# Gated DeltaNet heads: three GpSimd products taken out of the scan, and other places for weight splits and block copies

## The chip, the cores and the metric

One core of a Trainium2 chip. The metric is the device time of one execution in microseconds, the median over several. Five engines run their own instruction streams side by side and wait for each other through semaphores: TensorE (PE, matrix products), VectorE (DVE), ScalarE (ACT), GpSimd (POOL) and SyncE (SP), which here only issues transfers.

## The reference

One inference step of a hybrid network with two layers that share their shapes, over 512 latent and 128 context tokens of width 1024. A layer normalises its input, scales and shifts it, projects it, and hands the projection to four branches of four heads each: A (gated DeltaNet), B (Hyena convolution), C (neighbourhood attention), D (differential attention). Their outputs are gated, projected, merged and projected again. The change is in branch A alone:

```python
def gdn_chunked(q, k, v, g, beta, s0):
    gc = jnp.cumsum(g..., axis=-1)
    decay = jnp.where(incl, jnp.exp(gc_i - gc_j), 0.0)
    kb = k * beta
    lower = jnp.where(strict, einsum('id,jd->ij', kb, k) * decay, 0.0)
    sol = triangular_solve(lower + eye, concatenate([v * beta, kb * exp(gc)]))
    u, w = sol[..., :dv], sol[..., dv:]
    a_intra = jnp.where(incl, einsum('id,jd->ij', q, k) * decay, 0.0)
    q_dec, k_dec, g_last = q * exp(gc), k * exp(gc_last - gc), exp(gc_last)
    def step(s, xs):
        v_new = u_i - w_i @ s
        o_i = q_i @ s + a_i @ v_new
        s = s * gl_i + k_i.T @ v_new
        return s, o_i
```

q and k pass a width-3 convolution, SiLU and an L2 norm; v a convolution and SiLU. Each head runs it in both directions of the sequence (d = 0, 1), with initial states per head, and the final context states are an output.

## The kernel before, in words

Everything is written out by hand, engine by engine; no planner reorders it. Tokens are five tiles of 128 (four latent, one context); a chunk in the kernel is a tile. All large projections go through blocks of 128 output channels (8 x 128 x 128 weights, 512 KB). SP loads a block into one of two raw buffers (`stream`), ScalarE makes its rounded upper part (`split_hi`, called `A_hi` in branch A), VectorE the rest (`split_lo`, `A_lo`), and TensorE makes three products per piece (upper times upper, upper times rest, rest times upper) into one of two PSUM buffers `proj` (L794). A block of branch A is cut into eighths, which `eighths`, `fill` and `part` put as filling between the small steps of the Delta heads. A load waits until both splits of the block two before are done, a split until TensorE is through with the block two before it.

**A head** has four blocks (q, k, v, gate) and these stages. *Front* (units u = 0 to 9, TensorE into `mix`, ScalarE out of it, `A_front` on both): u 0 to 2 turn the log-decays and ScalarE makes `decT` = exp(-|gc_i - gc_j|) for both directions, 128 x 1280; u 3 to 5 turn k and q into token order and sum their squares; u 5 to 7 make the Gram products k k^T and k q^T (`gram`); u 8, 9 turn v. *Masks and blocks*: GpSimd's `A_front` takes the inverse roots of the sums of squares (`stat`, L600) and scales beta by them; then it makes three products of 128 x 1280: `dec` = decT * beta * rn^2, decT * triangle (L617), and that times the Gram matrix of q (L623). VectorE's `A_decays` and `A_blocks` cut the 16 x 16 diagonal blocks out (four 32 x 320 products each, into D32, then `C16`), and `A_lower` multiplies `dec` by the Gram matrix of k. *Block inverses*: the blocks travel by small transfers (`blocks_in`; tiles 0 to 2 through SP's queue in `relay`, tiles 3 and 4 through GpSimd's) to 40 partitions, where VectorE inverts all 16 x 16 blocks (`A_scaled`, `A_pivots` 1 to 14, `A_inverse`), and back (`inverses_back`). VectorE spreads direction 0 and ScalarE direction 1 into X and Y (`A_spread`). *Levels*: the inverse grows from 16 to 32 to 64 to 128 in steps on TensorE (`A_level_q`, `A_level_d`, `A_mid_q`, ...), each answered by ScalarE (`A_level`, `A_mid`, `A_last`) and VectorE (`update`, `update_mid`, `update_last`). *Scan*: five steps, `A_scan` on TensorE, ScalarE's copy of v (`vn`), VectorE's state update and output sums (`A_step`, L2504 and L2511).

The stages of neighbouring heads overlap: during the levels of head h (TensorE's `A_levels(h)`) ScalarE scales keys and values of head h (`A_keys`, 30 evictions of 128 x 128), units 0 to 2 of head h+1 are made, and 24 eighths are filled in; during the scan of head h units 3 to 9, the masks and the blocks of head h+1 are made, with up to eight eighths between (none in the scan of head 2). The first pivots of head h+1 are at the end of that scan, the others in its levels. After the last head comes the join, the merge of branch A, with the same kind of blocks.

SP issues its transfers in one order: in `unit_stream`, the load of block 4h+7 of branch A stands ahead of `relay(h)`, which waits for the blocks and then for the inverses of head h; the next loads come after it. GpSimd does, per head: store of the state, load of the next, its part of `inverses_back`, root of the output norm (`A_o_root`), zeroing of the output tile (`A_rest`), then `A_front(h+1)`.

Of the kernel before, what the change touches and what calls it, by code (L numbers as in the profile page):

```python
# [44 lines left out]
def program(nc, I, O):  # L45
# [3 lines left out]
    with ctx:  # L49
# [64 lines left out]
        stat = sb("stat", [128, 64])  # L114
# [183 lines left out]
        BETA_SQ, O_STAT = 40, 56  # L298
# [224 lines left out]
        def _(pool):  # L523
# [20 lines left out]
            for layer in range(DEPTH):  # L544
# [49 lines left out]
                beta_sq = stat[:, BETA_SQ:BETA_SQ + 10].rearrange("p (d t) -> p d t", d=2)  # L594

                def A_front(h):
                    roots = stat[:, 20 * (h % 2):20 * (h % 2) + 10]
# [5 lines left out]
                    pt(stat[:, 20 * (h % 2) + 10:20 * (h % 2) + 20], roots, roots)  # L603
# [3 lines left out]
                    pt(A_head(5, h), A_head(5, h), both(rn_k_sq(h)))  # L607
# [3 lines left out]
                    if h == 0:  # L611
                        P.memset(XT, 0.0)
                    decT = decTs[h % 2]
                    pool.wait_ge(A_own.sem, A_own.at(layer, 3 * h + 1))
                    held(pool)
                    pt(dec, decT, beta_sq.unsqueeze(3).to_broadcast([128, 2, TILES, 128])).then_inc(A_dm.sem, A_dm.step)
                    pt(decT, decT, A_mask(tri))  # L617
                    pool.wait_ge(A_own.sem, A_own.at(layer, 3 * h + 2))
                    held(pool)
                    P.drain()  # L620
                    for t in range(SP_TILES, TILES):
                        blocks_in(pool, t, A_relay_pool)
# [24 lines left out]
                for h in range(HEADS):  # L647
# [965 lines left out]
        def _(act):  # L1613
# [21 lines left out]
            for layer in range(DEPTH):  # L1635
# [94 lines left out]
                def A_front(h, u):  # L1730
# [19 lines left out]
                    elif u == 3:  # L1750
                        copy(A_tmv[:, 0:4, :], src(4))
                        for t in range(4):
                            last = squares(0, rn_k(h), t, t)
                    elif u == 4:
                        for t in range(4):
                            last = squares(1, rn_q(h), t, t)
                    elif u == 5:
                        copy(A_tmv[:, 4:5, :], src(1))
                        squares(0, rn_k(h), 4, 0)
                        squares(1, rn_q(h), 4, 1)  # L1760
                        copy(gram[:, 4, :, :], src(2, 2))
                        A.drain()
                        A.activation(rn_k(h), rn_k(h), ACT.Copy, bias=EPS)
                        last = A.activation(rn_q(h), rn_q(h), ACT.Copy, bias=128.0 * EPS, scale=128.0)
# [8 lines left out]
                def A_keys(h, out, i, d, x0=0):  # L1773

                    for t in range(TILES):
                        at = 40 * i + 20 * d + 5 * h + t
                        A.activation(out[:, d, t, :], A_tmv[:, x0 + t, :], ACT.Identity, scale=ab_s[:, at:at + 1])
# [73 lines left out]
                for u in (6, 7):  # L1851
                    A_front(0, u)
                A_silu_v(0)
                A_gate(0)
                A_hi(5)
                for u in (8, 9):
                    A_front(0, u)
                for h in range(HEADS):
                    more = h < HEADS - 1
                    if more:  # L1860
# [4 lines left out]
                        A_hi(4 * h + 7)  # L1865
                    else:
# [1368 lines left out]
```

## Time and profile before

| | us |
|---|---|
| median of 3 runs | 2523.73 (2523.3 to 2526.33) |
| the profiled execution | 2522.0 |
| its span in the trace | 2520.4 |
| TensorE busy, matmuls | 2371.7 (94%) |
| VectorE busy | 1371.6 (54%) |
| ScalarE busy | 1004.3 (40%) |
| GpSimd busy | 308.8 (12%) |

Branch A takes the stretch from about 60 to 375 us in layer 0, and from about 1300 to 1625 us in layer 1. "Idle before" in a timeline row is the time the engine stood still ahead of these instructions, with what released it. PEclk is the granted clock of TensorE, 1.00 for 2.4 GHz. L2247 (`tt`), L794 (`mm`), L1623 (`copy`), L580 (`pt`), L1777 (`A_keys`) are lines of helpers that several steps share, so the form and the tensor names tell the steps apart.

### The profile page before, as it was taken

To read this page: it belongs to the slowest core of one execution; us is meant where nothing else is said; L and a number is where in the kernel's file an instruction comes from. 1 tells how busy PE (TensorE), PEld (TensorE's weight loads), DVE (VectorE), ACT (ScalarE), POOL (GpSimd) and SP (SyncE) were. 2 spreads that over 40 slices of the span, in tenths; PEclk is the share of its full clock that TensorE was granted. 3 is DMA by queue.
4 is the path that set the end of the run, shared out by engine and by line. 5 is a ranking of instruction groups with operands and counts; after the bars stand their busy time and mean duration, and the time that the engine had idled before them with its cause. 6 is when DMAs were issued, how large, how long until landed. Compare 5 with 4: busy or idle time off the path is not lost. (4 is left out here: it accounts for less than half of the span.)

```text
span 2520.4 us, 49062 instructions
## 1 busy us (share of the span) xinstructions
PE 2371.7 (94%) x19072; PEld 2262.5 (90%) x19072; DVE 1371.6 (54%) x2553; ACT 1004.3 (40%) x2100; POOL 308.8 (12%) x438
## 2 busy tenths in 40 slices
PE   7888889999999999999998887999999999999998
PEld 5778779999999999999987776899999999999898
DVE  5576653677333425663556676537773344356644
ACT  4655433333234424442366554323332353255422
POOL 1222211000011101110012222100000110011000
PEclk9999899999999999999999988999999999999999
DMA  7110114111334323214221111231113332222132
GB/s 270 49 43 26 41 40 149 42 51 43 109 105 100 87 101 99 62 59 148 85 84 49 43 34 35 67 127 35 51 50 88 88 91 85 77 68 82 49 106 84
DMA packets 63262, 195.43 MB, mean 78 GB/s; under 512 B 16376, under 2 KB 16542, under 8 KB 62928
## 3 DMA queue, kind: packets, MB, share of 16 engines
q1 hardware_dynamic: 46880, 148.55, 17.8%
q0 software_dynamic: 16176, 44.07, 6.7%
q8 instruction: 138, 2.26, 0.4%
q14 instruction: 68, 0.56, 0.1%
HBM read 177.97 MB, written 8.39 MB: 74 GB/s over the span
## 5 line engine op out<-in xcount | busy, mean ns | idle before, releaser
L794 PE MATMUL proj<-h_hi,w_hi 128*128 128x320 f32 x3072 | 741.3, 322 | 20.8 <-issue 8.5
L794 PE MATMUL proj<-h_lo,w_hi 128*128 128x320 f32 x3072 | 706.2, 311 | 0.0
L794 PE MATMUL proj<-h_hi,w_lo 128*128 128x320 f32 x3072 | 702.0, 311 | 0.0
L2247 DVE TENSOR_TENSOR w_lo<-raw,w_hi 128x1024 fp32r<-128x1024 f32 x232 | 283.6, 1222 | 513.2 <-ACT w_hi L1623 512.1
L794 PEld LDWEIGHTS proj<-h_hi,w_hi 128*128 128x128 f32 x3072 | 510.1, 190 | 36.4 <-issue 22.9
L794 PEld LDWEIGHTS proj<-h_lo,w_hi 128*128 128x128 f32 x3072 | 519.3, 190 | 0.0
L794 PEld LDWEIGHTS proj<-h_hi,w_lo 128*128 128x128 f32 x3072 | 516.8, 189 | 0.0
L1623 ACT ACTIVATE w_hi<-raw 128x1024 fp32r<-128x1024 f32 x232 | 245.9, 1060 | 533.3 <-PE proj L794 329.7
L794 PE MATMUL mix<-area 128*128 128x128 f32 (+8 forms) x4576 | 400.1, 267 | 45.8 <-DVE area L2464 38.4
L794 PEld LDWEIGHTS mix<-area 128*128 128x128 f32 (+5 forms) x4576 | 339.4, 163 | 86.0 <-issue 59.8
L1623 ACT ACTIVATE area<-mix 128x384 f32<-128x384 f32 (+8 forms) x374 | 151.6, 426 | 583.3 <-PE mix L794 468.5
L2247 DVE TENSOR_TENSOR area<-area 128x512 f32<-128x512 f32 (+14 forms) x476 | 212.9, 464 | 62.4 <-ACT merged L2169 15.5
L1623 ACT ACTIVATE area<-proj 128x128 f32<-128x128 f32 (+8 forms) x248 | 80.8, 392 | 134.2 <-PE proj L794 124.8
L794 PE MATMUL mix<-y_hi,w_hi 128*128 128x320 f32 x512 | 120.7, 317 | 2.7 <-DVE merged L2247 1.7
L797 PE MATMUL mix<-ident,area 128*128 128x128 f32 x668 | 109.2, 281 | 9.8 <-DVE area L2247 2.6
L794 PE MATMUL mix<-y_hi,w_lo 128*128 128x320 f32 x512 | 116.7, 309 | 0.0
L794 PE MATMUL mix<-y_lo,w_hi 128*128 128x320 f32 x512 | 116.6, 309 | 0.0
L797 PEld LDWEIGHTS mix<-ident,area 128*128 128x128 f32 x668 | 79.1, 142 | 21.9 <-ACT area L1740 3.8
L794 PEld LDWEIGHTS mix<-y_hi,w_hi 128*128 128x128 f32 x512 | 84.1, 188 | 7.8 <-issue 5.2
L2247 DVE TENSOR_TENSOR area<-area,mix 128x384 f32<-128x384 f32 (+3 forms) x112 | 46.6, 455 | 77.1 <-ACT area L1623 77.1
L2924 DVE TENSOR_REDUCE stat<-mix 128x1 f32<-128x640 f32 (+1 forms) x80 | 56.7, 717 | 54.4 <-PE mix L794 42.7
L794 PEld LDWEIGHTS mix<-y_hi,w_lo 128*128 128x128 f32 x512 | 85.6, 188 | 0.0
(319 smaller groups left out, 2677.2 us busy)
## 6 DMA issues: line engine op xcount, KB each, us to landing
raw<-in_w_in SPq DMA_DIRECT2D x128, 512.0 KB, 3.5
raw<-in_w_mb SPq DMA_DIRECT2D x96, 512.0 KB, 3.5
raw<-in_w_mod POOLq DMA_DIRECT2D x32, 512.0 KB, 4.5
area<-in_bias POOLq DMA_DIRECT2D x64, 128.0 KB, 4.7
raw<-in_w_out SPq DMA_DIRECT2D x16, 512.0 KB, 3.5
out_x<-area SPq DMA_DIRECT2D x10, 512.0 KB, 2.6
merged<-in_w_mod SPq DMA_DIRECT2D x8, 512.0 KB, 11.2
area<-area POOLq DMA_DIRECT2D x64, 64.0 KB, 1.9
```

What stands on the lines that cost most here:

```text
L794: return T.matmul(out, l, r, start=start, stop=stop)
L797: return T.transpose(out, src, ident[:, :])
L1623: return A.activation(out, x, ACT.Copy, scale=scale)
L2247: return V.tensor_tensor(out, a_, b_, op)
L2924: V.tensor_reduce(stat[:, 2 * m + j:2 * m + j + 1], D_scores[j][:, first:NT], AX.X, ALU.max, negate=True).then_inc(Dd["mx"].sem, Dd["mx"]. ...
```

## The change

The first of the three products (decay rows times beta) goes: `dec` is now made by ScalarE (`A_gram_rows`, ten evictions of 128 x 128: the k Gram row of a tile times beta * rn^2), and VectorE's `A_lower` multiplies it by `decT` instead of by `gram`. VectorE makes the factor itself (`A_factor`, a reciprocal and one product). The other two products are in GpSimd's new `A_masked`: for heads 0 to 2 it runs in the levels of the same head, after its first update; for head 3 at the end of `A_front`, behind `A_lower`. GpSimd's block transfers in `A_front` no longer stand between products. `A_values` scales v by a column that GpSimd makes in `stat` (`beta_rn`), so the inverse roots and the raw sums have columns of their own. `A_hi(4h+9)` goes from ahead of the scan to its third step, `A_lo(4h+9)` behind `A_lower` in the third step, `A_decays(h+1)` behind the first step; `A_take(h+1, 1)` ahead of the keys; `A_lo(4h+7)` behind all pivots and `A_inverse`; the first convolution of head h+1 behind `A_spread`.

```diff
@@ GpSimd
 def A_front(h):
     pool.wait_ge(A_fev.sem, A_fev.at(layer, FRONT * h + 6))
-    P.tensor_tensor(roots, roots, neg_half[:, 0:10], ALU.pow)
+    P.tensor_tensor(roots, stat[:, SUMS:SUMS + 10], neg_half[:, 0:10], ALU.pow)
...
+    pt(squares, roots, roots)
+    pt(beta_rn, A_head(1, h), both(rn_k(h)))
...
-    pt(beta_sq, A_head(1, h), both(rn_k_sq(h)))
     pt(A_head(5, h), A_head(5, h), both(rn_k_sq(h))).then_inc(A_rn.sem, A_rn.step)
-    pt(A_head(1, h), A_head(1, h), both(rn_k(h))).then_inc(A_rn.sem, A_rn.step)
     if h == 0:
         P.memset(XT, 0.0)
-    pool.wait_ge(A_own.sem, A_own.at(layer, 3 * h + 1))
-    pt(dec, decT, beta_sq.unsqueeze(3).to_broadcast([128, 2, TILES, 128])).then_inc(A_dm.sem, A_dm.step)
-    pt(decT, decT, A_mask(tri))
     pool.wait_ge(A_own.sem, A_own.at(layer, 3 * h + 2))
     for t in range(SP_TILES, TILES):
         blocks_in(pool, t, A_relay_pool)
+    if h == HEADS - 1:
+        A_masked(h)
+
+def A_masked(h):
+    decT = decTs[h % 2]
+    if h == HEADS - 1:
+        pool.wait_ge(A_lat.sem, A_lat.at(layer, h + 1))
+    else:
+        pool.wait_ge(A_x.sem, A_x.at(layer, 5 * h + 2))
+    pt(decT, decT, A_mask(tri))
     P.drain()
     pt(decT, decT, A_both(gram[:, :, 1, :])).then_inc(A_dm.sem, A_dm.step)
@@ GpSimd, loop over heads
     if h:
         A_o_root(h - 1)
+    if h < HEADS - 1:
+        A_masked(h)
     if h:
         pool.wait_ge(A_ot.sem, A_ot.at(layer, h))
@@ ScalarE
+def A_values(h):
+    for d in range(2):
+        for t in range(TILES):
+            A.activation(Rv[:, d, t, :], A_tmv[:, TILES + t, :], ACT.Identity, scale=beta_rn[:, d, t:t + 1])
+
+def A_gram_rows(h, d):
+    if d == 0:
+        act.wait_ge(A_own.sem, A_own.at(layer, 3 * h + 1))
+        A.drain()
+    for t in range(TILES):
+        last = A.activation(dec[:, d, t, :], gram[:, t, 0, :], ACT.Identity, scale=beta_sq[:, d, t:t + 1])
+    if d:
+        last.then_inc(A_dm.sem, A_dm.step)
@@ ScalarE, before head 0
     for u in (6, 7):
         A_front(0, u)
+    A_gram_rows(0, 0)
+    A_gram_rows(0, 1)
+    A_hi(5)
     A_silu_v(0)
     A_gate(0)
-    A_hi(5)
@@ ScalarE, head h
         A_hi(4 * h + 7)
+        A_take(h + 1, 1)
...
     for d in range(2):
         A_keys(h, Rk, 5, d)
-    for d in range(2):
-        A_keys(h, Rv, 1, d, TILES)
-    if more:
-        A_take(h + 1, 1)
+    A_values(h)
...
-        A_hi(4 * h + 9)
     for n, units in enumerate(((), (3, 4, 5), (6, 7), (8,), (9,))):
+        if more and n == 2:
+            A_hi(4 * h + 9)
+        if more and n == 3:
+            A_gram_rows(h + 1, 1)
         for u in units if more else ():
             A_front(h + 1, u)
+        if more and n == 2:
+            A_gram_rows(h + 1, 0)
         act.wait_ge(A_va.sem, A_va.at(layer, 5 * h + n + 1))
@@ VectorE
+def A_factor(h):
+    dve.wait_ge(A_fev.sem, A_fev.at(layer, FRONT * h + 6))
+    fence()
+    V.reciprocal(stat[:, INV:INV + 5], sums_k)
+    fence()
+    mul(beta_sq, ab_s[:, 40:80]...[:, :, h, :], stat[:, INV:INV + 5]...).then_inc(A_own.sem, A_own.step)
 def A_blocks(h):
     dve.wait_ge(A_fev.sem, A_fev.at(layer, FRONT * h + 8))
-    dve.wait_ge(A_rn.sem, A_rn.at(layer, h + 1))
 def A_lower(h):
     dve.wait_ge(A_dm.sem, A_dm.at(layer, 2 * h + 1))
     for d in range(2):
-        last = mul(dec[:, d], dec[:, d], gram[:, :, 0, :])
+        last = mul(dec[:, d], dec[:, d], decTs[h % 2][:, d])
@@ VectorE, before head 0
     A_convolve(0, 2)
+    A_decays(0)
+    A_factor(0)
     A_lo(4)
-    A_decays(0)
     A_blocks(0)
@@ VectorE, head h
-    A_pivots(4, 9)
+    A_pivots(4, 15)
+    A_inverse(h)
     A_lo(4 * h + 7 if more else 18)
-    A_pivots(9, 15)
-    A_inverse(h)
-    if more:
-        A_convolve(h + 1, 0)
     if h:
         A_out_squares(h - 1)
     A_spread(h)
     if more:
+        A_convolve(h + 1, 0)
         A_convolve(h + 1, 1)
...
-    if more:
-        A_lo(4 * h + 9)
-    else:
+    if not more:
         A_lo(19)
     dve.wait_ge(A_rest.sem, A_rest.at(layer, h + 1))
-    if more:
-        A_decays(h + 1)
     for n in range(5):
         A_step(h, n)
...
-        if n == 1:
+        if n == 0:
+            A_decays(h + 1)
+            A_factor(h + 1)
+        elif n == 1:
             A_blocks(h + 1)
         elif n == 2:
             A_lower(h + 1)
+            A_lo(4 * h + 9)
         elif n == 3:
             A_scaled(h + 1)
             A_pivots(1, 4)
```

## Rows read from the trace of the kernel before

**Rows 1.** The page, its head: busy us (share of the span) and instructions.

```profile
span 2520.4 us, 49062 instructions
...
PE 2371.7 (94%) x19072; PEld 2262.5 (90%) x19072; DVE 1371.6 (54%) x2553; ACT 1004.3 (40%) x2100; POOL 308.8 (12%) x438
```

**Rows 2.** TensorE's waits, whole span: engine, line <- releaser: total, times, longest.

```profile
PE mix L794 <- DVE area L2464: 38.4, 8, 6.2
...
PE mix L794 <- DVE area L2504: 29.2, 18, 4.3
```

**Rows 3.** TensorE's timeline, layer 0: start, length, instructions [idle before <- releaser].

```profile
92.05 0.53 PE L794 MATMUL proj<-h_hi,w_hi 128*128 128x320 f32 x2 [3.59 <-issue]
...
153.68 0.49 PE L794 MATMUL mix<-merged,area 128*128 128x128 f32 x2 [3.42 <-DVE area L2504]
...
180.51 0.53 PE L794 MATMUL proj<-h_hi,w_hi 128*128 128x320 f32 x2 [1.26 <-ACT area L1623]
...
185.51 2.40 PE L794 MATMUL mix<-area 64*64 64x64 f32 x40 [3.89 <-DVE area L2464]
```

**Rows 4.** Windows: stretch, length, busy of each engine, PEclk, DMA share, GB/s.

```profile
92.05:96.60 4.55, 4.55 (x22) 4.54 (x23) 0.22 (x1) 2.18 (x8) 3.25 (x2) 0.62 0.57 160
154.60:158.00 3.40, 3.40 (x16) 3.30 (x15) 3.40 (x2) 0.67 (x2) 3.30 (x2) 0.50 0.17 26
276.00:302.00 26.00, 17.92 (x114) 15.85 (x112) 20.83 (x42) 10.59 (x38) 12.32 (x10) 0.86 0.08 24
```

**Rows 5.** VectorE's groups by form, 137 to 164 us: busy, mean ns | idle.

```profile
L2247 DVE TENSOR_TENSOR area<-area,gate_sg 32x320 f32<-32x320 f32 x4 | 5.6, 1398 | 0.3 <-ACT gate_sg L1623 0.3
L2247 DVE TENSOR_TENSOR area<-area,gate_sg 128x640 f32<-128x640 f32 x2 | 4.7, 2397 | 0.0
L2504 DVE SCALAR_TENSOR_TENSOR area<-area,ab_s,mix 128x128 f32<-128x128 f32 x8 | 2.4, 344 | 2.6 <-PE mix L794 2.3
...
L2247 DVE TENSOR_TENSOR area<-area,blocks 32x320 f32<-32x320 f32 x4 | 1.9, 483 | 0.0
```

**Rows 6.** GpSimd's timeline, front of head 1.

```profile
145.55 2.33 POOL L580 TENSOR_TENSOR area<-area,stat 128x1280 f32<-128x1280 f32 x1
147.84 3.16 POOL L580 TENSOR_TENSOR area<-area,tri 128x1280 f32<-128x1280 f32 x1
...
154.98 2.93 POOL L580 TENSOR_TENSOR area<-area,gate_sg 128x1280 f32<-128x1280 f32 x1
```

**Rows 7.** VectorE's timeline: before head 0 (three), levels of head 1 (three).

```profile
89.26 1.55 DVE L2247 TENSOR_TENSOR area<-area,gate_sg 128x640 f32<-128x640 f32 x2
90.73 1.22 DVE L2247 TENSOR_TENSOR w_lo<-raw,w_hi 128x1024 fp32r<-128x1024 f32 x1
96.38 1.28 DVE L2247 TENSOR_TENSOR area<-area 40x256 f32<-40x256 f32 x3 [4.42 <-DMA area<-area]
...
175.05 3.56 DVE L2247 TENSOR_TENSOR area<-area 40x108 f32<-40x108 f32 x12
...
184.42 0.94 DVE L2464 TENSOR_SCALAR area<-area,blocks 128x160 f32<-128x160 f32 x4
...
196.65 1.32 DVE L2486 COPY area<-mix 32x160 f32<-32x160 f32 x4 [2.62 <-PE mix L794]
```

**Rows 8.** ScalarE's timeline: before head 0 (one), levels of head 1 (three).

```profile
79.15 0.60 ACT L1623 ACTIVATE gate_sg<-mix 128x512 f32<-128x512 f32 x1 [0.62 <-PE mix L794]
...
169.61 0.63 ACT L1737 ACTIVATE area<-mix,ab_s 128x128 f32<-128x128 f32 x2 [1.65 <-PE mix L797]
...
173.71 5.96 ACT L1777 ACTIVATE merged<-area,ab_s 128x128 f32<-128x128 f32 x20
...
184.42 1.41 ACT L1785 ACTIVATE area<-area,blocks 128x160 f32<-128x160 f32 x4 [1.13 <-DMA area<-area]
```

**Rows 9.** SP's queue: issues of the block copies, there and back.

```profile
92.50 2.15 SPq L284 DMA_DIRECT2D area<-area  x3
...
179.77 2.40 SPq L287 DMA_DIRECT2D area<-area  x3
```

More of the change, by code:

```diff
@@ L297, in program @@
                         for d in range(2) for i in range(2))
-        BETA_SQ, O_STAT = 40, 56
+        BETA_SQ, BETA_RN, O_STAT, INV, SUMS = 40, 50, 60, 65, 70
+        beta_sq, beta_rn = (stat[:, at:at + 10].rearrange("p (d t) -> p d t", d=2) for at in (BETA_SQ, BETA_RN))
+        sums_k, sums_q = stat[:, SUMS:SUMS + 5], stat[:, SUMS + 5:SUMS + 10]
         rn_k, rn_q, rn_k_sq, rn_q_sq = (lambda h, i=i: stat[:, 20 * (h % 2) + 5 * i:20 * (h % 2) + 5 * i + 5] for i in range(4))
@@ L592, in both @@
                     return v.unsqueeze(1).to_broadcast([128, 2, TILES])
[L594 removed]
                 def A_front(h):
[L597 removed]
+                    roots, squares = (stat[:, 20 * (h % 2) + i:20 * (h % 2) + i + 10] for i in (0, 10))
                     pool.wait_ge(A_fev.sem, A_fev.at(layer, FRONT * h + 6))
                     held(pool)
[L600 removed]
+                    P.tensor_tensor(roots, stat[:, SUMS:SUMS + 10], neg_half[:, 0:10], ALU.pow)
@@ L601, in A_front @@
                     held(pool)
                     P.drain()
-                    pt(stat[:, 20 * (h % 2) + 10:20 * (h % 2) + 20], roots, roots)
+                    pt(squares, roots, roots)
+                    pt(beta_rn, A_head(1, h), both(rn_k(h)))
                     held(pool)
                     P.drain()
-                    pt(beta_sq, A_head(1, h), both(rn_k_sq(h)))
-                    pt(A_head(5, h), A_head(5, h), both(rn_k_sq(h)))
+                    pt(A_head(5, h), A_head(5, h), both(rn_k_sq(h))).then_inc(A_rn.sem, A_rn.step)
@@ new lines, in A_front @@
+                    if h == 0:
+                        P.memset(XT, 0.0)
+                    pool.wait_ge(A_own.sem, A_own.at(layer, 3 * h + 2))
+                    held(pool)
+                    for t in range(SP_TILES, TILES):
+                        blocks_in(pool, t, A_relay_pool)
+                    if h == HEADS - 1:
[6 more added lines that the diff above has]
+                        pool.wait_ge(A_x.sem, A_x.at(layer, 5 * h + 2))
+                    held(pool)
+                    pt(decT, decT, A_mask(tri))
@@ L617, in A_front @@
-                    pt(decT, decT, A_mask(tri))
[L618 to L622, printed above, removed]
                     pt(decT, decT, A_both(gram[:, :, 1, :])).then_inc(A_dm.sem, A_dm.step)
@@ L1752, in A_front @@
                         for t in range(4):
-                            last = squares(0, rn_k(h), t, t)
+                            last = squares(0, sums_k, t, t)
                     elif u == 4:
                         for t in range(4):
-                            last = squares(1, rn_q(h), t, t)
+                            last = squares(1, sums_q, t, t)
                     elif u == 5:
                         copy(A_tmv[:, 4:5, :], src(1))
-                        squares(0, rn_k(h), 4, 0)
-                        squares(1, rn_q(h), 4, 1)
+                        squares(0, sums_k, 4, 0)
+                        squares(1, sums_q, 4, 1)
                         copy(gram[:, 4, :, :], src(2, 2))
                         A.drain()
-                        A.activation(rn_k(h), rn_k(h), ACT.Copy, bias=EPS)
-                        last = A.activation(rn_q(h), rn_q(h), ACT.Copy, bias=128.0 * EPS, scale=128.0)
+                        A.activation(sums_k, sums_k, ACT.Copy, bias=EPS)
+                        last = A.activation(sums_q, sums_q, ACT.Copy, bias=128.0 * EPS, scale=128.0)
                     elif u < 8:
@@ L1771, in A_front, with A_keys @@
                     last.then_inc(A_fev.sem, A_fev.step)
-                def A_keys(h, out, i, d, x0=0):
+                def A_keys(h, out, i, d):
                     for t in range(TILES):
                         at = 40 * i + 20 * d + 5 * h + t
-                        A.activation(out[:, d, t, :], A_tmv[:, x0 + t, :], ACT.Identity, scale=ab_s[:, at:at + 1])
+                        A.activation(out[:, d, t, :], A_tmv[:, t, :], ACT.Identity, scale=ab_s[:, at:at + 1])
+                def A_values(h):
[10 more added lines that the diff above has]
+                        last.then_inc(A_dm.sem, A_dm.step)
                 cols = lambda at, n: M[:, at:at + 5 * n].rearrange("p (t c) -> p t c", c=n)
@@ L2423, in A_decays @@
                     for c, w in QUARTERS:
-                        last = mul(D32[c], decTs[h % 2][c, :, :, c], lower_16[c].unsqueeze(1).unsqueeze(1).to_broadcast([32, 2, TILES, 32]))
-                    last.then_inc(A_own.sem, A_own.step)
+                        mul(D32[c], decTs[h % 2][c, :, :, c], lower_16[c].unsqueeze(1).unsqueeze(1).to_broadcast([32, 2, TILES, 32]))
+                def A_factor(h):
[3 more added lines that the diff above has]
+                    fence()
+                    mul(beta_sq, ab_s[:, 40:80].rearrange("p (d h t) -> p d h t", d=2, h=HEADS)[:, :, h, :],
+                        stat[:, INV:INV + 5].unsqueeze(1).to_broadcast([128, 2, TILES])).then_inc(A_own.sem, A_own.step)
                 def A_blocks(h):
                     dve.wait_ge(A_fev.sem, A_fev.at(layer, FRONT * h + 8))
-                    dve.wait_ge(A_rn.sem, A_rn.at(layer, h + 1))
                     fence()
@@ L2611, in _ @@
                     A_spread(h)
+                    if more:
+                        A_convolve(h + 1, 0)
                     if more:
```

8 lines of the change are left out of this document (2 added, 6 removed).

## The prediction

> **What bounds the kernel now.** I read the page's busy times first: TensorE is busy in 94% of a span of 2520.4 us, no other engine in more than 54% [rows 1]. Time is therefore to be had in two ways only: where TensorE stands still, and where it runs at the lower of its two clocks. The list of waits says where it stands still [rows 2]: 38.4 us in 8 waits for L2464 (`A_spread`, ahead of the first level step of each Delta head) and 29.2 us in 18 waits for L2504 (the state update of a scan step). TensorE's timeline then gives the places in layer 0 [rows 3]: 3.59 us ahead of 92.05, before the first head's levels; 3.42 ahead of 153.68, the fourth scan step of head 0; 1.26 ahead of 180.51, a projection tile not yet emptied; 3.89 ahead of 185.51, the spread. Layer 1 repeats them: 3.46 before the first head. The same scan step waits 3.42, 2.86, 3.07 and 2.84 us in the four scans of heads 0 and 1, and twice 4.26 in those of head 2; these six make 20.7 of the 29.2 us. After the longer waits the granted clock falls [rows 4]: it is 0.50 (1.2 GHz) in 154.60 to 158.00, in all of which TensorE is busy, and 0.62 in 92.05 to 96.60. 3.4 us at 0.50 would take 1.7 at 1.0, 4.55 at 0.62 would take 2.8: 1.7 lost at each.
>
> Why the fourth step is late stands in VectorE's groups and GpSimd's timeline [rows 5, 6]. The four 32x320 products of `A_blocks` take 5.6 us, four of the same form in `A_decays` 1.9; the two 128x640 products of `A_lower` take 4.7, against 1.55 with GpSimd idle [rows 7]. GpSimd runs its products from 145.55 to 151.0 and from 154.98 to 157.9; VectorE's products with both operands in SBUF stand still under them. The state updates (one operand in PSUM) have a mean of 344 ns over all eight, so those weren't held.
>
> **A. Ahead of head 0 (two).** Before, `A_blocks` and `A_lower` under GpSimd push `A_lo(5)` to 90.73 to 91.95 [rows 7], and TensorE waits for it. After, blocks cost 1.9 plus 0.6 for the beta copy and the addition, from 79.9 (gram copied at 79.75, [rows 8]) to 82.5. ScalarE's ten gram rows cost 3.0 (20 of that form take 5.96), until 82.9; `A_lower` ends at 84.5, `A_lo(5)` at 85.7, 2.8 us before TensorE asks (92.05 - 3.59 = 88.46). `A_silu_v(0)`, now behind the gram rows, ends near 85.9, just as TensorE wants to turn the values: 0.2 off. (3.59 + 1.7 - 0.2) + (3.46 + 1.7 - 0.2) = 10.0.
>
> **B. Scans of heads 0 and 1 (four).** `A_hi` (1.05) leaves the way of the first step on ScalarE, `A_lo` (1.2) and `A_decays` (1.9) on VectorE, so fronts 3 to 5 come 0.7 earlier. The third step is where ScalarE gets fuller. On head 0's clock: copy of v for step 2 ends at 142.1, `A_hi` 143.2, gram copies 145.8 (TensorE delivers the last at 145), five gram rows 147.5 (5 x 0.30), copy of v 147.9; TensorE has own work until 148.0. It fits by 0.1. `A_factor` (two fences, two tiny instructions, 0.8) stands behind `A_decays` and is done at 143.0, before ScalarE asks at 145.8. `A_blocks` ends at 148.5 and not 152.9, so the state update ends at 149.2, and TensorE comes at 149.6. The wait goes in all four, 12.2, and the low clock with it, 6.8. Four small waits of 0.36 to 0.38 a scan: half of them, 3.0. `A_lower` (150.2 to 151.8) and `A_lo` (to 153.0) now stand before the next update, wanted at 154.0: no stall; the last step waits 0.4 for the output sum, 1.6 off. 12.2 + 6.8 + 3.0 - 1.6 = 20.4.
>
> **B'. Scan of head 2 (two).** No projection work fills it: TensorE is busy 17.92 of 26 us, at a mean clock of 0.86 [rows 4]. The bare chain is copy of v (0.4), products (1.0), state update (0.7), products (1.0), with what stands in front on each engine. I get the state-dependent products of steps 2 to 5 at 280.0, 284.4, 288.6, 292.9 in place of 281.5, 285.8, 293.2, 299.6, and the next levels at 295 in place of 302.1. The third step hardly gains, since `A_hi` and five gram rows are before its copy of v; `A_lo(17)` ahead of the fourth update costs 1.9. 7.0 each, 14.0.
>
> **C. Level stages (eight).** `A_inverse` no longer stands behind `A_lo(4h+7)`, which waits 3.5 us for ScalarE. The 12 instructions of pivots 9 to 14 (3.56, [rows 7]) follow at 170.4, the inverse (1.0) ends at 175.0 instead of 179.7; the copies took 4.7 from there to 184.42, so VectorE can spread at 179.7. But ScalarE does the other direction [rows 8], and from 169.61 on it is full: front 0.6, table load 1.3, Exp 1.3, split 1.0, take 0.7, keys 5.96 and 3.03, until 183.3; before its spread it is idle only 1.13. So what is late next is ScalarE. Direction 1 of `A_level_q` can start at 184.7; before, direction 0 started at 185.51 and direction 1 1.2 later. 2.0 each in heads 0 and 1, 2.3 in head 2 (idle 1.46), 12.6 for six. The 1.26 us for the tile goes too (`A_take(h+1, 1)` moves ahead of the keys), but is inside this, as ScalarE ends the stage either way. Head 3 has 0.8 idle to lose, and 0.8 of the first direction: 1.6 each. 12.6 + 3.2 = 15.8.
>
> **What is added.** `A_masked(h)` (3.16 + 2.93 us, [rows 6]) runs in the levels of heads 0 to 2 from the first update on, at 192.0 on head 1's clock. Behind it on VectorE: two COPY_PREDICATED of the other direction, then `A_lo(4h+8)` (two SBUF operands: held until 194.9, ends 196.1), which delays nothing, as `update_mid` waits 2.62 for TensorE until 196.65 [rows 7]. The second product ends at 199.1, beside the CAST of y at 199.04 (0.1), the zeroing of o at 199.8, wanted at 201.7. Cost 0. The COPY_PREDICATED (mask in SBUF, data in PSUM) are the unknown: no row has one under a reading GpSimd product. Nearest rows: the state updates (SBUF and PSUM) aren't held at all; `A_blocks` is held to the end of the product [rows 5]. So 0 at one end; at the other the first waits for product 1 and the second for product 2, 5.8 a head, 35 in six. I take 0, the row nearer in operands.
>
> The Trainium skill ("SBUF — State Buffer", Who interferes with whom) says that a VectorE instruction with at most one SBUF input, outside the two-port modes, doesn't contend with GpSimd. By that the copies go free and the sum stands; by the opposite it would be 35 less. No row here shows it for this instruction.
>
> SP: the load of block 4h+11 waits for `A_lo(4h+9)`, and the block copies of head h+1 stand behind it in SP's queue. They go at 153.1 with a load before them. Head 0 shows the price already: copies issued 92.50 to 94.65 behind a load at 92.05, VectorE on its way at 96.38 after an idle 4.42 [rows 7, 9]. So `A_scaled(h+1)` starts near 157.4 and, through pivots, inverse and copies, the spread at 175, on a stage in which ScalarE needs until 179. Cost 0, cover 4. If the cover went, each further microsecond is one a head. For head 3 the masked products run in head 2's scan and can hold `A_scaled` 1.8 more: inside the cover.
>
> **Sum.** 10.0 + 20.4 + 14.0 + 15.8 = 60.2. It is made against the profiled execution, 2522.0 (span 2520.4), 1.7 below the median of 2523.73. For the median: 2523.7 - 60.2 = 2463.5, say 2464.
>
> **Rivals.**
> 1. ScalarE ends the scan steps (gram rows ahead of v in steps 3 and 4). For: a fit by 0.1. Against: TensorE's filling. Price at most ten rows, 3.0 a scan, six scans 18: 2482.
> 2. The predicated copies are held. For: the mask comes from SBUF. Against: the updates' 344 ns. 35: 2499, less where TensorE has filling, 2496.
> 3. The clock rises everywhere: waits at the spread of 1 to 2 us in place of 3.9 to 6 leave no stretch at 0.50. Against: two waits remain, one for each direction. 1.7 to 2 more a head, 15: 2449.
> 4. Slower: GpSimd holds every VectorE instruction of the level chain, those that read PSUM too (second update, `update_mid`, y, `update_last`), and the zeroing of o comes late. Products 6.1, `A_lo` 1.2, a low-clock stretch 1.7, one more instruction held, 1.7: 10.7 a head, 64 in six: 2528. It decides from 10.0 a head (60.2 / 6). Against: the 344 ns again.
> That the products still run beside the blocks would need `A_masked` to slip into the scan; only head 3 does so, behind `A_lower`: then B' halves, 2471, inside the range.
>
> **Chances.** Forecast (2454 to 2474) 0.45; rival 1 0.22; rival 2 0.15; rival 3 0.12; rival 4 or no gain 0.06. Range 2448 to 2500, about 0.05 left out on either side. No change is within 0.2% (5 us), about what can be told from none. Faster 0.94, same 0.02, slower 0.04.
>
> **What would show it.** Right: no wait ahead of head 0's levels; `A_blocks` products of 0.49 us; no wait over 0.5 us for L2504's successor in heads 0 and 1; ScalarE without idle before its spread, and TensorE waiting for it between the directions. Wrong: a predicated copy over 2 us; ScalarE's copy of v as the last releaser; `A_scaled` so late that the spread comes after ScalarE's keys; a clock of 0.50 still behind every scan.

## Result and the profile after

The changed kernel takes 2458.72 us, median of 4 runs (2458.35 to 2459.11), against 2524.46 (2523.3 to 2526.33) for the kernel before: ratio 0.9739, 95% interval 0.9722 to 0.9756. That is 65.7 us less. The span fell by 63.3 us, from 2520.4 to 2457.1, and the mean granted clock rose from 0.978 to 0.987. The forecast was 60.2 less, 2464.

The head of the page answers to [rows 1]:

```profile
span 2457.1 us, 49168 instructions
PE 2353.1 (96%) x19072; PEld 2247.7 (91%) x19072; DVE 1344.5 (55%) x2569; ACT 1026.6 (42%) x2180; POOL 293.3 (12%) x422
```

TensorE's waits by line answer to [rows 2]; L2495 is the spread (L2464 before), L2535 the state update (L2504 before), L1629 ScalarE's copies and L1805 its spread:

```profile
PE mix L800 <- DVE area L2495: 26.0, 8, 3.7
PE mix L800 <- ACT area L1629: 5.4, 8, 1.3
PE mix L800 <- DVE area L2535: 3.2, 2, 1.6
PE mix L800 <- ACT area L1805: 2.6, 5, 0.8
```

The state update made TensorE wait 29.2 us in 18 waits and makes it wait 3.2 in 2. The spread went from 38.4 to 26.0, in 8 waits as before, and is now by far the largest. Of TensorE's waits over 2 us in branch A (the fourth scan step, ahead of head 0's levels, the spread), only those at the spread are left.

TensorE's timeline in layer 0 answers to [rows 3]: the spread of head 0, the fourth scan step of head 0, the two directions of head 1's first level, and three steps in the scan of head 2.

```profile
108.70 1.54 PE L800 MATMUL mix<-area 64*64 64x64 f32 x24 [3.37 <-DVE area L2495]
...
142.78 0.49 PE L800 MATMUL mix<-merged,area 128*128 128x128 f32 x2
...
170.18 1.33 PE L800 MATMUL mix<-area 64*64 64x64 f32 x20 [2.77 <-DVE area L2495]
171.91 1.33 PE L800 MATMUL mix<-area 64*64 64x64 f32 x20 [0.40 <-ACT area L1805]
...
264.12 0.71 PE L800 MATMUL mix<-area,merged 128*128 128x128 f32 x4 [1.27 <-ACT area L1629]
...
270.07 0.71 PE L800 MATMUL mix<-merged,area 128*128 128x128 f32 x4 [1.59 <-DVE area L2535]
271.35 0.79 PE L800 MATMUL mix<-area,merged 128*128 128x128 f32 x4 [0.56 <-ACT area L1629]
```

The row at 142.78 has no bracket: the fourth step waits for nothing, where it waited 3.42. In the windows (answering to [rows 4]) the clock shows the same. Ahead of head 0's levels it is 1.00 with no idle (9.00 of 9.00), and behind a spread wait of about 3 us it is still 0.50:

```profile
88.00:97.00 9.00, 9.00 (x66) 8.98 (x66) 5.18 (x17) 6.96 (x17) 0.00 (x0) 1.00 0.13 41
108.00:112.00 4.00, 3.30 (x44) 3.21 (x45) 3.78 (x8) 2.32 (x9) 0.00 (x0) 0.50 0.49 181
171.00:175.00 4.00, 3.60 (x36) 3.03 (x33) 3.78 (x6) 2.89 (x9) 0.00 (x0) 0.50 0.11 46
```

VectorE's timeline answers to [rows 5, 7]. First the levels of head 0 (update under GpSimd's product), then the scan (blocks, lower, scaled), then the spread:

```profile
115.29 0.52 DVE L2511 COPY_PREDICATED area<-level,mix 128x320 f32<-128x320 uint8 x1 [1.96 <-PE mix L800]
...
116.45 0.52 DVE L2511 COPY_PREDICATED area<-level,mix 128x320 f32<-128x320 uint8 x1 [0.25 <-PE mix L800]
116.87 0.51 DVE L2512 COPY_PREDICATED area<-level,mix 128x320 f32<-128x320 uint8 x1
117.27 3.14 DVE L2272 TENSOR_TENSOR w_lo<-raw,w_hi 128x1024 fp32r<-128x1024 f32 x1
...
139.22 1.98 DVE L2272 TENSOR_TENSOR area<-area,gate_sg 32x320 f32<-32x320 f32 x4 [0.26 <-ACT gate_sg L1629]
...
143.73 1.55 DVE L2272 TENSOR_TENSOR area<-area 128x640 f32<-128x640 f32 x2
...
151.42 1.27 DVE L2272 TENSOR_TENSOR area<-area 40x256 f32<-40x256 f32 x3 [3.03 <-DMA area<-area]
...
169.09 0.94 DVE L2495 TENSOR_SCALAR area<-area,blocks 128x160 f32<-128x160 f32 x4 [1.24 <-DMA area<-area]
```

GpSimd's two products of head 0, in the levels now ([rows 6] had them in the scan), and SyncE's transfers of head 1 (answering to [rows 9]): block copies at 146.95, behind a load, and inverse copies.

```profile
116.39 2.95 POOL L582 TENSOR_TENSOR area<-area,tri 128x1280 f32<-128x1280 f32 x1 [11.16 <-DVE area L2512]
119.66 3.54 POOL L582 TENSOR_TENSOR area<-area,gate_sg 128x1280 f32<-128x1280 f32 x1 [0.33 <-issue]
```

```profile
146.50 0.33 SPq L437 DMA_DIRECT2D raw<-in_w_in  x1
146.95 2.02 SPq L284 DMA_DIRECT2D area<-area  x3
164.53 2.40 SPq L287 DMA_DIRECT2D area<-area  x3
```

ScalarE's timeline answers to [rows 8]: the first set of gram rows in the scan of head 0 with the copy of v behind it, then the run into its spread of head 1, the keys and values without idle between them.

```profile
139.10 1.57 ACT L1795 ACTIVATE area<-gate_sg,stat 128x128 f32<-128x128 f32 x5
140.58 0.36 ACT L1629 ACTIVATE area<-mix 128x256 f32<-128x256 f32 x1
...
161.67 3.04 ACT L1783 ACTIVATE merged<-area,ab_s 128x128 f32<-128x128 f32 x10
164.61 3.04 ACT L1788 ACTIVATE merged<-area,stat 128x128 f32<-128x128 f32 x10
167.54 3.02 ACT L1783 ACTIVATE merged<-area,ab_s 128x128 f32<-128x128 f32 x10
170.46 1.40 ACT L1805 ACTIVATE area<-area,blocks 128x160 f32<-128x160 f32 x4
```

**A ruler for the stages.** Two kinds of TensorE product mark a head: the first `mix<-area,merged` behind its levels, and the next `mix<-ident,ab_s`, some 4 us behind the scan's last product. From the first to the second I call "scan", from the second to the next head's first mark "levels" (projection units, pivots, spread and level steps). "Last" is from head 2's first mark to head 3's, its scan and the last levels together. Means of both layers, in us, worked out from the starts in each trace; idle and low clock (granted clock under 1) are summed in the same stretches, where the text needs them:

| kernel | scan, heads 0, 1 (four) | levels, heads 1, 2 (four) | last (two) |
|---|---|---|---|
| before | 32.4 | 38.2 | 68.6 |
| after | 26.2 | 35.6 | 60.6 |
| e1_small_products | 27.0 | 37.9 | 60.9 |
| e2_order_only | 32.4 | 36.1 | 67.8 |
| e3_products_back | 32.0 | 36.0 | 65.0 |
| e4_masks_in_scan | 26.2 | 35.8 | 60.5 |
| e5_blocks_first | 26.2 | 35.6 | 60.8 |
| e6_keys_later | 26.2 | 34.7 | 61.0 |
| e7_both | 26.2 | 31.9 | 59.5 |
| e8_rows_twice | 28.2 | 35.8 | 62.0 |
| e9_head2_scan | 26.2 | 32.6 | 59.0 |

### The profile page after: what moved, and what is told of

It is laid out like the page before. It is cut to its first block and busy times, and to the rows that moved or that the text cites. A ratio compares the mean times of both kernels' runs of the same rounds, so it can differ in the third digit from the quotient of the medians.

```text
span 2457.1 us, 49168 instructions
## 1 busy us (share of the span) xinstructions
PE 2353.1 (96%) x19072; PEld 2247.7 (91%) x19072; DVE 1344.5 (55%) x2569; ACT 1026.6 (42%) x2180; POOL 293.3 (12%) x422
## 5 line engine op out<-in xcount | busy, mean ns | idle before, releaser
L2272 DVE TENSOR_TENSOR w_lo<-raw,w_hi 128x1024 fp32r<-128x1024 f32 x232 | 294.9, 1271 | 455.2 <-ACT w_hi L1629 454.2
L1629 ACT ACTIVATE w_hi<-raw 128x1024 fp32r<-128x1024 f32 x232 | 245.9, 1060 | 533.9 <-PE proj L800 330.5
L800 PE MATMUL mix<-area 128*128 128x128 f32 (+8 forms) x4576 | 394.8, 265 | 35.7 <-DVE area L2495 26.0
L800 PEld LDWEIGHTS mix<-area 128*128 128x128 f32 (+5 forms) x4576 | 333.7, 161 | 77.1 <-issue 47.8
L1629 ACT ACTIVATE area<-mix 128x384 f32<-128x384 f32 (+8 forms) x374 | 152.1, 425 | 523.7 <-PE mix L800 424.2
L2272 DVE TENSOR_TENSOR area<-area 128x512 f32<-128x512 f32 (+14 forms) x492 | 228.7, 483 | 79.3 <-DMA area<-area 30.3
L1629 ACT ACTIVATE area<-proj 128x128 f32<-128x128 f32 (+8 forms) x248 | 80.9, 393 | 134.1 <-PE proj L800 124.8
L803 PE MATMUL mix<-ident,area 128*128 128x128 f32 x668 | 108.1, 279 | 10.3 <-DVE area L2272 2.6
```

Of the source, the lines that this page charges most:

```text
L800: return T.matmul(out, l, r, start=start, stop=stop)
L803: return T.transpose(out, src, ident[:, :])
L1629: return A.activation(out, x, ACT.Copy, scale=scale)
L2272: return V.tensor_tensor(out, a_, b_, op)
```

## Experiments

Each was timed in 3 rounds beside the kernel before on the same chip, the last in 5. For the first four, before took 2524.51 us (7 runs); for the next four 2523.65 (7 runs); for the last 2523.04 (9 runs).

### The products alone, and the order alone

Of the kernel before, with GpSimd's three products made small (it leaves out that part of the computation: `dec` is zero, and the masks reach 8 of 128 columns of a tile):

```diff
-    pt(dec, decT, beta_sq...).then_inc(A_dm.sem, A_dm.step)
-    pt(decT, decT, A_mask(tri))
+    P.memset(dec, 0.0).then_inc(A_dm.sem, A_dm.step)
+    pt(decT[:, :, :, 0:8], decT[:, :, :, 0:8], tri[:, :, 0:8]...)
...
-    pt(decT, decT, A_both(gram[:, :, 1, :])).then_inc(A_dm.sem, A_dm.step)
+    pt(decT[:, :, :, 0:8], decT[:, :, :, 0:8], gram[:, :, 1, 0:8]...).then_inc(A_dm.sem, A_dm.step)
```

> The kernel before, with GpSimd's work taken down and nothing moved: the first product is replaced by a zeroing of dec (a write only), the triangle and the Gram product run over 8 of 128 columns per tile. This leaves out that part of the computation. Theory (VectorE's products of two SBUF operands stood still under GpSimd's reads): A_blocks products at 0.49 us each, the wait ahead of head 0's levels and the 2.8 to 4.3 us waits of the fourth scan step go, with their low clock: 10 + 19 + 12 = about 41 us, 2483. Rival (the gain came from the new places of splits, decays and inverse): under 15 us, 2510 or more.

Measured: 2477.49 us, ratio 0.9818 [0.9802, 0.9835], 47 less. The scans fell by 5.4, the last stretch by 7.7, the levels by 0.3. VectorE's four products of `A_blocks` take 2.15 us in the scan of head 0, against 5.6 before:

```profile
143.83 2.15 DVE L2247 TENSOR_TENSOR area<-area,gate_sg 32x320 f32<-32x320 f32 x4 [0.29 <-ACT gate_sg L1623]
```

So the products did hold the scans, by what they held of VectorE, and with the old order of everything else.

Of the kernel before, with the order of the levels alone:

```diff
-    A_pivots(4, 9)
+    A_pivots(4, 15)
+    A_inverse(h)
     A_lo(4 * h + 7 if more else 18)
-    A_pivots(9, 15)
-    A_inverse(h)
-    if more: A_convolve(h + 1, 0)
     if h: A_out_squares(h - 1)
     A_spread(h)
+    if more: A_convolve(h + 1, 0)
@@ ScalarE: A_take(h + 1, 1) directly behind A_hi(4 * h + 7), not behind the keys
```

> The kernel before, with the order in the levels alone changed: A_inverse straight after all pivots and ahead of A_lo(4h+7), the convolution behind the spread, A_take(h+1, 1) ahead of the keys. GpSimd's products stay where they were. Theory (ScalarE ends the level stage, with 1.1 to 1.8 us of idle to lose and direction 0 made in the meantime): 2.0 us a head and 1.6 in head 3, 12 to 16 us, 2510. Rival (the levels gain only once the scan delivers the blocks earlier): 0 to 4 us.

Measured: 2510.86 us, ratio 0.9948 [0.9931, 0.9965], 13.7 less. The scans stayed at 32.4, and the levels fell by 2.1. TensorE's timeline at head 1's first level shows what is late next, just as the forecast had it: direction 0 comes early, and direction 1 waits for ScalarE's spread, which starts at 182.30.

```profile
179.99 0.80 PE L794 MATMUL mix<-area 64*64 64x64 f32 x20 [0.73 <-DVE area L2463]
183.76 0.80 PE L794 MATMUL mix<-area 64*64 64x64 f32 x20 [2.98 <-ACT area L1785]
```

The two add up to 47.0 + 13.7 = 60.7 of the 65.7.

### The products put back

Of the changed kernel, with GpSimd's time in the scan given back by products that nothing needs:

```diff
+    for _ in range(4):
+        P.drain()
+        pt(area[:, 16160:16800]..., strict[:, 0, :]..., tri[:, 0, :]...)
     pool.wait_ge(A_own.sem, A_own.at(layer, 3 * h + 2))
```

> The changed kernel with four extra GpSimd products of 128 x 640 per head (constants into unused memory, 6 us together) where the three stood before, ahead of its block transfers. Theory (the lock): A_blocks is held for about 4 to 5 us again in every scan and ahead of head 0, 38 us back, 2497. Rival (placement): GpSimd has the time, so under 10 us, 2459 to 2468.

Measured: 2500.1 us, ratio 0.9908 [0.9891, 0.9924]: 41 more than after. The scans are back at 32.0, the last stretch at 65.0, and the levels at 36.0. In the scan of head 0 GpSimd's four extra products take 6.82 us and end at 149.6; `A_blocks` beside them takes 6.43 in place of 1.98 and ends 0.3 us later, and the wait of the fourth scan step is back (VectorE's row, then TensorE's):

```profile
143.51 6.43 DVE L2276 TENSOR_TENSOR area<-area,gate_sg 32x320 f32<-32x320 f32 x4 [0.27 <-ACT gate_sg L1633]
```

```profile
151.29 0.65 PE L804 MATMUL mix<-merged,area 128*128 128x128 f32 x2 [4.19 <-DVE area L2539]
```

With the order, the queues and ScalarE's rows of the changed kernel, GpSimd's reading products alone undo the gain in the scans. In this kernel `A_scaled` waits less for its transfer (1.47 us, against 3.03), so it isn't GpSimd's later block copies that bring the time back.

### The masked products in the scan after all

```diff
     for t in range(SP_TILES, TILES):
         blocks_in(pool, t, A_relay_pool)
-    if h == HEADS - 1:
-        A_masked(h)
+    A_masked(h)      # waits A_lat(h + 1) for every head; gone from the levels
```

> The changed kernel with A_masked(h) for all heads where head 3 has it: in GpSimd's A_front behind A_lower, so in the scan (head 0: ahead of its levels), not in the levels. Theory: what counts is that the products don't run under A_blocks and A_lower; behind A_lower they hold A_lo(4h+9) or A_scaled, by 1 to 2 us, under the 3 us that A_scaled waits for its blocks anyway, and A_lo(4h+8) in the levels is free again: 2456 to 2464. Rival (the levels were the only place with room): A_lo(4h+9), now ahead of a state update, is held by 3 us in four scans and the update with it, 12 to 20 us, 2475.

Measured: 2460.81 us, ratio 0.9751 [0.9735, 0.9767]: 2 more than after. Which of these two places the products have is worth nothing to speak of; that they don't run beside `A_blocks` and `A_lower` is what pays. It also prices what they cost in the levels: nothing, as forecast, since taking them out of there brings no gain (35.8 a level, against 35.6).

### What is left at the spread

SyncE's order: block copies ahead of the load of unit 4h+7.

```diff
+def relay_blocks(h):      # the block copies, split off from relay(h)
...
 def unit_stream(u):
+    if u % UNIT == 3 and u > 3:
+        relay_blocks(u // UNIT - 1)
@@ merge, block 3
+    if b == 0 and j == 3: relay_blocks(HEADS - 1)
```

> The changed kernel, with one order changed on SyncE's queue: the block copies of head h (A_scaled needs them) are issued ahead of the load of weight unit 4h+7, not behind it. It takes away A_scaled's wait of 3.03 us in the fourth scan step. My theory of what is left: each head's levels wait some 3 us at the spread for two engines that end within 0.4 us of each other, VectorE (spread of direction 0 from 169.09, whose last releaser is a DMA) and ScalarE (spread of direction 1 from 170.46, no idle ahead of it); taking one away alone leaves the other. Expected 2450 to 2458, against 2458.7. Rival: VectorE alone sets the wait, and direction 1 follows for nothing: some 2.4 us in each of six heads and the half-clock time behind them, 2440 or less.

ScalarE's order: the keys `kd` beside the levels.

```diff
     A_values(h)
-    act.wait_ge(A_sb.sem, A_sb.at(layer, 5 * h))
-    for d in range(2): A_keys(h, kd, 3, d)
...
+    act.wait_ge(A_sb.sem, A_sb.at(layer, 5 * h))
+    A_keys(h, kd, 3, 0)
     A_mid(h)
     A_last(h)
+    A_keys(h, kd, 3, 1)
```

> The changed kernel, with ScalarE's ten copies of kd (3.04 us) moved from ahead of its spread to beside the levels: five ahead of A_mid, five behind A_last. Theory: VectorE's spread stays where it is, held by the transfers of the inverse, so only the 0.4 to 0.8 us between the directions go, and the five ahead of A_mid may cost that back: 2454 to 2461. Rival: ScalarE sets the wait: 2445 or less.

Both diffs together:

> Both edits of the two kernels before in one. Theory: only now the wait at the spread goes from about 3 us to about 1 in six heads (heads 0 excepted), with direction 1 close behind, 2.0 to 2.4 us each, and the stretches at the low clock behind them shrink: 12 to 20 us, 2438 to 2447, clearly more than the two alone add up to. Rival: the two are independent, and the sum of the two alone is what comes; or VectorE's chain of pivots is the true bound, and nothing comes: 2452 or more.

Measured: e5 2460.22 us (ratio 0.975 [0.9732, 0.9767]), 1.5 more than after; e6 2453.49 (0.9719 [0.9703, 0.9735]), 5 less; e7 2434.66 (0.9644 [0.9628, 0.966]), 24 less than after, and 89 less than before. Alone they bring -1.5 and 5, together 24. The four runs of e5 spread from 2456.57 to 2463.45, so its 1.5 can't be told from nothing. All three came out just outside the theory's figures (2450 to 2458, 2454 to 2461, 2438 to 2447), but far from the rivals': neither edit alone frees the wait, and the two aren't independent. TensorE's first level of head 1 in e5, e6 and e7, in this order:

```profile
167.48 0.80 PE L807 MATMUL mix<-area 64*64 64x64 f32 x20 [0.76 <-DVE area L2502]
171.22 0.80 PE L807 MATMUL mix<-area 64*64 64x64 f32 x20 [2.95 <-ACT area L1812]
```

```profile
169.25 1.38 PE L800 MATMUL mix<-area 64*64 64x64 f32 x40 [2.25 <-DVE area L2495]
```

```profile
163.78 1.62 PE L807 MATMUL mix<-area 64*64 64x64 f32 x40 [0.77 <-DVE area L2502]
```

With SyncE's edit alone the wait for VectorE falls from 2.77 to 0.76 and comes back in the next row, for ScalarE. With ScalarE's edit alone direction 1 waits for nothing (one row of 40 products), and direction 0 still waits for a transfer. With both, 0.77 is left. In the four levels of heads 1 and 2 the idle time falls from 3.5 to 4.1 us to 1.5 to 2.8, and the low clock from 3.4 to 6.8 us to none. By the means, 1.9 us a level is waiting, and the 4.3 us that ran at half speed cost 2.1; together that is the 3.7 that the levels lost, give or take 0.3. At head 3's spread nothing is won: TensorE waits 3.2 and 3.4 us there in e7's two layers.

### How full ScalarE is in the scan

Of the changed kernel, each set of five gram rows issued twice:

```diff
     for t in range(TILES):
+        A.activation(dec[:, d, t, :], gram[:, t, 0, :], ACT.Identity, scale=beta_sq[:, d, t:t + 1])
+    A.drain()
+    for t in range(TILES):
         last = A.activation(dec[:, d, t, :], gram[:, t, 0, :], ACT.Identity, scale=beta_sq[:, d, t:t + 1])
```

> The changed kernel, with ScalarE's five copies of gram rows (1.57 us) issued twice for each direction (3.2 us more on ScalarE in the scan's third step and 1.6 more in its fourth, in place of what GpSimd's product did there before). It asks how near the change came to making ScalarE the engine that ends a scan step (the prediction's first rival). Theory: in heads 1 and 2's making ScalarE is ready some 2 us before the v copy is wanted, so 1.6 us more in a step cost 0 to 1 us in each of two steps of six scans, together with low clock at most: 2459 to 2468. Rival: ScalarE already ends the steps and each copy counts in full, 3.2 us in each of six scans: 2478 or more.

Measured: 2480.05 us, ratio 0.9827 [0.981, 0.9845]: 21 more than after, and so above the theory's 2459 to 2468 and at the rival's 2478. (The edit puts 1.6 us into the third step and 1.6 into the fourth, not 3.2 and 1.6 as the expectation has it.) By the marks of the profiled executions 8 of it are in the four scans (1.9 each), 6 ahead of the first marks of the two layers, where the same rows stand before head 0, 3 in the last stretches and 1 in the levels. This row of TensorE, in the scan of head 0, has 1.16 of the 1.9:

```profile
146.40 0.71 PE L800 MATMUL mix<-area,merged 128*128 128x128 f32 x4 [1.16 <-ACT area L1629]
```

1.6 us more ahead of a copy of v give 1.16 of waiting, so the third step of the changed kernel had 0.4 us to spare. The trace of the changed kernel has the same: the copy of v ends at 140.94, and TensorE's products that need it start at 141.32. Not each copy counts in full (that would be 3.2 a scan), so the rival's number came without its mechanism, with 6 us from ahead of head 0 that neither had counted; but the slack of 2 us in my expectation was not there.

### A further step that brought nothing

The kernel of e7_both, with the split of unit 17 moved in head 2's scan:

```diff
@@ ScalarE, step n of the scan
-    if more and n == 2: A_hi(4 * h + 9)
+    if more and n == 2 and h < 2: A_hi(4 * h + 9)
...
+    if n == 4 and h == 2: A_hi(17)
     act.wait_ge(A_va.sem, A_va.at(layer, 5 * h + n + 1))
@@ VectorE
     A_lower(h + 1)
-    A_lo(4 * h + 9)
+    if h < 2: A_lo(4 * h + 9)
...
+    if h == 2: A_lo(17)
     A_scaled(h + 1)
```

> The kernel of e7_both, and in the scan of head 2 alone the two halves of the split of weight unit 17 moved: ScalarE's (1.04 us) from ahead of the v copy of step 3 to its idle time ahead of the last v copy (2.91 us there), VectorE's (1.22 us) from ahead of the update of step 4 to behind it, ahead of A_scaled, which waits for a transfer and then under GpSimd's product anyway. TensorE waited 1.27 and 1.59 us there in each layer. Theory: both waits fall to some 0.3 us, and A_scaled ends where it did: 4 to 5 us in the two layers, with a stretch at the low clock behind them 4 to 8: 2427 to 2431. Rival: the splits are late for the products of unit 17, or A_scaled is later by the 1.2 us and the spread wait of head 3 takes it back: 2433 or more.

Measured: 2433.34 us, median of 5 (2432.18 to 2437.38), ratio 0.965 [0.9637, 0.9663]: no difference from e7 that could be told. The state update's wait did fall, from 1.59 to 0.46 us, the one for the copy of v not at all, and a new wait came ahead of the products of unit 18. TensorE's timeline:

```profile
253.91 0.71 PE L807 MATMUL mix<-area,merged 128*128 128x128 f32 x4 [1.27 <-ACT area L1636]
...
258.74 0.71 PE L807 MATMUL mix<-merged,area 128*128 128x128 f32 x4 [0.46 <-DVE area L2544]
...
278.25 0.53 PE L807 MATMUL proj<-h_hi,w_hi 128*128 128x320 f32 x2 [3.03 <-ACT w_hi L1636]
```

The row names ScalarE's split, but these products wait for both halves of the split of unit 18. ScalarE's half starts at 268.9 in e9 and in e7 and ends well before; the half that ends 0.1 us ahead of the products is VectorE's, `A_lo(18)`, which stands behind all pivots and the inverse (e9 first, then e7 with TensorE's row behind its split):

```profile
262.07 4.04 DVE L2281 TENSOR_TENSOR area<-area 40x256 f32<-40x256 f32 x3
...
276.94 1.21 DVE L2281 TENSOR_TENSOR w_lo<-raw,w_hi 128x1024 fp32r<-128x1024 f32 x1
```

```profile
258.31 4.72 DVE L2279 TENSOR_TENSOR area<-area 40x256 f32<-40x256 f32 x3
...
273.90 1.21 DVE L2279 TENSOR_TENSOR w_lo<-raw,w_hi 128x1024 fp32r<-128x1024 f32 x1
```

```profile
275.21 0.53 PE L807 MATMUL proj<-h_hi,w_hi 128*128 128x320 f32 x2
```

On both kernels' own clocks, from the products of the third step on (253.91 and 251.41), TensorE is through with unit 17 after 21.3 us in place of 23.8, and VectorE's split after 24.2 in place of 23.7. What TensorE gained it then waits, because `A_scaled` and all that hangs on it start later behind the moved `A_lo(17)`. That is the rival of the expectation: VectorE's chain takes it back.

## Why the prediction was right

By the ruler of the stages, the terms of the sum against what the two traces show:

| term | forecast | measured |
|---|---|---|
| A and head 0's levels (two) | 10.0 + 4.0 | 13.5 (6.1 and 7.4) |
| B, scans of heads 0 and 1 (four) | 20.4 | 24.6 |
| C, levels of heads 1 and 2 (four) | 8.6 | 10.3 |
| B' and head 3's levels (two) | 14.0 + 3.2 | 16.1 |
| rest of the span | 0 | -1.2 |
| sum | 60.2 | 63.3 |

**A.** Right: no wait ahead of head 0's levels and a full clock there.

**B.** The mechanism was right, and the size too small, by 1.0 us a scan. The four products of `A_blocks` take 1.98 us instead of 5.6 and the two of `A_lower` 1.55 instead of 4.7, and the wait of the fourth step is gone in all four scans. TensorE's idle time in a scan fell from 4.6 to 5.3 us to 1.0 to 1.1, by 3.8 on average, where the forecast's terms (3.05 for the wait, 0.75 for half of the small ones, less 0.4 at the last step) make 3.4. The 3.4 us of low clock are gone in all four, 1.7. That makes 5.5 of 6.1.

The remaining 0.6 is neither idle nor low clock in the trace, and e1, which kept the old order, lacks it. Laid side by side product by product, e1 and the changed kernel differ in the first two steps of the scan. In e1 `A_decays` stands ahead of the first state update on VectorE, and TensorE waits for that update in the second step, as it does before:

```profile
138.54 0.49 PE L794 MATMUL mix<-merged,area 128*128 128x128 f32 x2 [0.38 <-DVE area L2504]
```

The changed kernel has no such wait. The first products behind one also start 0.21 us apart in place of 0.11, which the trace counts as busy. No run moved `A_decays` alone.

One step of the forecast came right in size by luck: "and the low clock with it, 6.8". In the second layer of e2, whose scans have the order and the held products of before, the clock stayed at 1.00 behind the wait of the fourth step, and the scan was no shorter (32.4 and 32.2 us, as before). From the fourth step's products to the fifth's it is 6.39 us there and 6.38 before, where the clock was low (e2 first, then before):

```profile
1394.26 0.49 PE L794 MATMUL mix<-merged,area 128*128 128x128 f32 x2 [3.05 <-DVE area L2503]
...
1400.65 0.71 PE L794 MATMUL mix<-merged,area 128*128 128x128 f32 x4 [1.85 <-DVE area L2503]
```

```profile
1400.06 0.49 PE L794 MATMUL mix<-merged,area 128*128 128x128 f32 x2 [3.07 <-DVE area L2504]
...
1406.44 0.71 PE L794 MATMUL mix<-merged,area 128*128 128x128 f32 x4 [0.41 <-DVE area L2504]
```

With the full clock TensorE only waits 1.85 us in place of 0.41, for the update that stands behind `A_lower` (4.70 us there). In this stretch the low clock by itself cost nothing. The 1.7 us a scan came because `A_lower` was no longer held and gave 3.2 us back at the same place, which the forecast's sum has no term for.

**B'.** Right in size with head 3's levels (16.1 of 17.2). Shifted to the shorter clock (22.4 us earlier at the start of this scan), the forecast put the last state-dependent products at 292.9 - 22.4 = 270.5; they start at 270.07. The 1.59 ahead of them is the `A_lo(17)` that the forecast had priced at 1.9.

**C.** The cause was right and a step inside it wrong. e2 shows the forecast picture whole: VectorE early, ScalarE late, direction 1 waiting 2.98. In the changed kernel the wait is 2.77 for VectorE and only 0.40 for ScalarE, because the two spreads start close together: VectorE's at 169.09, 1.4 us ahead of ScalarE's at 170.46. The step that failed is "Cost 0, cover 4": the cover was 1.4. VectorE's side of it came as forecast. On the forecast's clock (6.4 us later, by the first marks at 132.03 and 125.67) the block copies go out at 153.3 (forecast 153.1), `A_scaled` starts at 157.8 (157.4), the spread at 175.5 (175). ScalarE was the one that came sooner, at 176.8 in place of 179. Its forecast end of 183.3, less the 5.1 that B gave a scan, would be 178.2, and less the 6.4 that this scan gave, 176.9. So 1.3 us of the miss are the larger gain in the scan, and 0.8 lie between that 178.2 and the 179 that the forecast used. The cost was 0 all the same, since ScalarE ends the stage either way: e5 took the delay away and the levels stayed at 35.6. What that miss hid was the next gain: the two ends lie so close that only both together free it (e7). The levels gave 2.6 on average and not 2.15; e2 has 2.1 from the order alone. The other 0.5 goes with the clock: levels with 3.4 us of low clock behind the spread take 35.5 to 35.6 us in both kernels, those with 6.8 take 35.9 to 36.4, and e2 has three of these in four, the changed kernel one.

**What was added** cost nothing. The unknown of the forecast, COPY_PREDICATED under a reading product of GpSimd, is settled: 0.52 us at 116.45 with the product running from 116.39, and 0.52 at 115.29 ahead of it. All twelve such copies that ran beside a product, in six heads, took 0.50 to 0.53; rivals 2 and 4 fall with this. The row that the forecast leaned on showed less than it said: in [rows 5], 137 to 164 us, none of the eight state updates ran beside a product. Those that did stand elsewhere in the trace before, and took the same (0.34 us each, at 214.68 and 285.10). The `w_lo` split at 117.27 is held (3.14 us instead of 1.2) and delays nothing. That is as the Trainium skill has it ("SBUF — State Buffer", Who interferes with whom): outside the two-port modes a VectorE instruction with at most one input in SBUF doesn't contend with GpSimd, one with two SBUF inputs does while GpSimd reads. The trace agrees, with 0.52 us for the copy (mask in SBUF, data in PSUM) and 3.14 for the split with both inputs in SBUF.

**Rival 1** (ScalarE ends the scan steps) was nearer than its 0.22 said to being a cost: there were 0.4 us to spare in the third step (e8), against the 0.1 of the forecast. It did not come true, and nothing but these tenths kept it away. **Rival 3** (the clock rises everywhere) needed the spread waits gone; at 3 us each they still leave 0.50 behind them in the rows at 108 and 171. In e7 both go together in heads 0 to 2, where waits of 0.8 to 1.8 us have no low clock behind them; at head 3's spread both stay.

## What to carry to other kernels

Where one engine's products hold another's, look for a place for them beside work with an operand in PSUM, or behind the held work: both did equally well here (e4), and most of the gain hangs on it (e1, e3). When a stage ends with a wait, read the idle time ahead of every engine that ends it, not only of the one the wait names: here VectorE and ScalarE ended within 1.4 us of each other, either repair alone brought -1.5 or 5 us, and both 24. An engine's slack in a step is measured best by doubling its instruction there (e8). Before a split is moved later, look at the chain behind it on the same engine (e9), and check the name that a wait gives against the end of everything the instruction waits for. And before a low clock is priced, ask what the engine would wait for next if it ran faster (e2).

## What the runs showed of the hardware that was not expected

- GpSimd's power of a 10-element column takes 2.0 to 2.3 us (135.20 in the changed kernel, 2.24), its 640-element product against broadcasts 1.7 (6.82 for four, e3): the small instruction is the longer.
- A wait of TensorE of 2.77 us is followed by 4 us at the granted clock 0.50, one of 0.77 us (e7) by none. But the length of the wait doesn't settle it: in the second layer of e2 waits of 3.44, 3.05 and 2.83 us were followed by the clock at 1.00. The 3.4 to 6.8 us at 0.50 behind the spreads of heads 1 and 2 cost TensorE 1.7 to 3.4 us each time; whether the kernel gets longer by it depends on what TensorE waits for next (in the scans of before it didn't).
